# Transposing the normalised x tiles of blocks two to five by DMA instead of on TensorE, in a hybrid short-convolution and chunk-MLP step

## The reference, cut to what matters

```
h = rms_norm(x, g_norm) * (1 + scale) + shift          # scale, shift, gate from silu(c) @ w_ada + b_ada
p = h @ w_in                                           # (T, 1024) @ (1024, 3584)
h_a, b_a, c_a, z_a, u_b, v_b, z_b = split(p, 7 x 512)
s   = c_a * h_a
y_a = b_a * causal_conv3(s) * silu(z_a)                # depthwise, along T
v_n = layer_norm(v_b, g_v, b_v)
y_b = u_b * (tril(W_s) @ v_n + b_s) * silu(z_b)        # in chunks of 128 positions, 8 heads
x + gate * (concat(y_a, y_b) @ w_out)  -> rms_norm(., g_final)
```

## Time and profile before

| | us |
|---|---|
| median of 3 runs | 351.91 (351.71 to 354.35) |
| the profiled execution, time | 349.13 |
| its span, slowest core | 347.5 (345.2 to 347.5) |
| PE busy | 293.0 (84% of the span) |
| DVE busy | 186.2 (54%) |
| ACT busy | 121.5 (35%) |
| POOL busy | 117.3 (34%) |

### The profile page before, as it was taken

The page is one execution under the profiler, slowest core; times in us unless marked ns, Lnnn a source line. Parts: engine busy times, 40 slices in busy tenths (PEclk is TensorE's granted clock), DMA queues, the critical chain, the costliest instruction groups (busy, mean ns, idle before and its releaser), DMA issues.

```text
span 347.5 us, 5602 instructions; the slowest of 8 cores (345.2 to 347.5 us)
## 1 busy us (share of the span) xinstructions
PE 293.0 (84%) x1767; PEld 152.8 (44%) x1792; DVE 186.2 (54%) x348; ACT 121.5 (35%) x215; POOL 117.3 (34%) x163
## 2 busy tenths in 40 slices
PE   0327469997999999999999999999999999989720
PEld 0213234444444445444454444455554567845300
DVE  0321025366464654657777655678734577586552
ACT  2511033128353227323455353345342323313120
POOL 7291264123424242412254241224202222232430
PEclk9999859999899999999999999999999999999875
DMA  5999999999999923480163515013540015071313
GB/s 142 222 166 173 165 169 159 185 234 219 171 211 199 164 80 91 119 271 8 60 182 77 167 25 182 2 60 122 122 122 22 10 62 156 27 215 58 123 61 123
DMA packets 14158, 44.52 MB, mean 128 GB/s; under 512 B 1968, under 2 KB 2352, under 8 KB 13104
## 3 DMA queue, kind: packets, MB, share of 16 engines
q0 software_dynamic: 6624, 21.24, 33.6%
q1 hardware_dynamic: 7504, 22.91, 21.8%
HBM read 51.02 MB, written 8.85 MB: 172 GB/s over the span
## 4 chain that ended last, share of the span: by engine, by line
PE 65%; DMA 11%; DVE 8%; issue 6%; POOL 5%; ACT 2%; DVEq 1%; POOLq 0%; ACTq 0%
PE pb L477 37%; PE pb L702 16%; DMA wada<-wada_l 11%; PE pb L592 8%; PE pb L403 1%; PE pb L654 1%; DVE st L607 1%; PE pb L789 1%; ACT vn_bf L622 1%; DVE tmp L532 1%; DVE ob L721 1%; DVE xn L389 1%; DVE spad L514 1%; POOL ob L721 1%; POOL xa L314 1%
## 5 line engine op out<-in xcount | busy, mean ns | idle before, releaser
L477 PE MATMUL pb<-hT,win_bf 128*128 128x512 bf16 (+3 forms) x672 | 127.0, 344 | 0.8 <-ACT vn_bf L622 0.4
L477 PEld LDWEIGHTS pb<-hT,win_bf 128*128 128x128 bf16 x680 | 66.4, 99 | 56.7 <-issue 3.0
L702 PE MATMUL pb<-wout_bf,yT 128*128 128x512 bf16 (+1 forms) x263 | 61.8, 387 | 4.4 <-POOL stat L768 2.1
L477 PE MATMUL pb<-hT,wh 128*128 128x512 bf16 (+3 forms) x276 | 55.4, 362 | 3.7 <-ACT hT L419 3.6
L551 POOL TENSOR_TENSOR yT<-tmp,tmp 128x512 bf16<-128x512 f32 (+3 forms) x20 | 24.7, 1235 | 60.4 <-DVE tmp L546 40.7
L723 ACT ACTIVATE junk<-ob 128x1024 bf16<-128x1024 f32 (+1 forms) x16 | 16.9, 1057 | 80.5 <-DVE ob L721 50.9
L674 POOL TENSOR_TENSOR yT<-tmp,tmp 128x512 bf16<-128x512 f32 (+3 forms) x20 | 22.9, 1147 | 62.5 <-DVE tmp L664 46.0
L702 PEld LDWEIGHTS pb<-wout_bf,yT 128*128 128x128 bf16 (+1 forms) x272 | 26.0, 100 | 34.3 <-issue 6.2
L477 PEld LDWEIGHTS pb<-hT,wh 128*128 128x128 bf16 x280 | 28.2, 102 | 29.0 <-issue 10.0
L532 DVE SCALAR_TENSOR_TENSOR tmp<-spad,pv,tmp 128x512 f32<-128x512 f32 (+2 forms) x40 | 26.7, 667 | 20.4 <-ACT tmp L525 13.1
L592 PE MATMUL pb<-wv_bf,hT 128*128 128x512 bf16 (+1 forms) x132 | 29.6, 379 | 0.2
(11 more groups left out here) (87 smaller groups left out, 270.4 us busy)
## 6 DMA issues: line engine op xcount, KB each, us to landing
y_p<-ob SPq DMA_DIRECT2D x15, 512.0 KB, 2.7
xc<-x_p SPq DMA_DIRECT2D x14, 512.0 KB, 7.7
wada<-wada_l POOLq DMA_DIRECT2D x6, 1024.0 KB, 33.7
xa<-x_p POOLq DMA_DIRECT2D x10, 512.0 KB, 35.0
win_bf<-win_l POOLq DMA_DIRECT2D x17, 256.0 KB, 38.4
xa<-x_p SPq DMA_DIRECT2D x8, 512.0 KB, 6.4
wout_bf<-wout_l POOLq DMA_DIRECT2D x2, 1024.0 KB, 53.3
wh<-winh_l POOLq DMA_DIRECT2D x4, 256.0 KB, 25.4
```

Of the source, the lines that this page charges most:

```text
L477: ii = pe.matmul(bk.t[:, 0:B.N], lhsT=wsl(m, k), rhs=hT[B.h][:, k, 0:B.N], start=(k == 0), stop=(k == 7))
L702: ii = pe.matmul(bk.t[R, :], lhsT=yT[B.y][:, k, ti * 128:ti * 128 + P], rhs=wout_bf[:, n, k, :], start=(k == 0), stop=(k == 7))
```

## The change

For blocks two to five `prep2` is no longer called. A new function `prep2d` issues one DMA on the SP queue that reads `xn` and writes the block's part of `hT` transposed, from SBUF to SBUF. `prep_xn` calls it right behind the DVE instruction; for the first tile of blocks four and five that is left out and the call comes at the end of the block's loop. Block one keeps PE's transposition. The resources that the DMA is recorded as writing are those of the copies before it: the tile's own, and the eight `hTk` that all tiles of a block share.

```diff
-    def prep_xn(B, i):
+    def prep_xn(B, i, now=True):
...
         pst[(B.i, i)] = rn
+        if B.i > 0 and now:
+            prep2d(B, i)
+
+    def prep2d(B, i):
+        ti, P, kind = B.tiles[i]
+        rn = pst[(B.i, i)]
+        dst = hT[B.h][:, :, ti * 128:ti * 128 + P]
+        op("sp", lambda e: e.dma_start(out=dst, in_=xn[rn][0:P, :], transpose=True),
+           r=[("xn", rn)], w=[("hT", B.h, i)] + [("hTk", B.h, k) for k in range(8)], dma=True)
...
             elif j == 3 and b == 1:
                 nxp(prep_sq, 2)
-                nxp(prep2, 0, "act")
...
             if not late:
-                nxp(prep2, j, "act")
                 nxp(prep_xn, j + 1)
...
             if b == 1 and j == 3:
-                nxp(prep2, 1, "act")
                 nxp(prep_xn, 2)
...
             if j == 3 and N2 is not None and b > 0:
-                prep_xn(N2, 0)
+                prep_xn(N2, 0, False)
             GB(B, j)
             if b == 0 and j == 0:
-                nxp(prep2, 0, "act")
-                nxp(prep2, 1, "dve")
...
-            if b == 0 and j == 1:
-                nxp(prep2, 2, "act")
-                nxp(prep2, 3, "dve")
...
             if b == 1 and j < 2:
-                nxp(prep2, 2 + j, "act")
...
+        if N2 is not None and b > 0:
+            prep2d(N2, 0)
```

## The result

The changed kernel takes 391.07 us (387.94 to 392.59, 4 runs) against 352.25 for the kernel before, run beside it: a ratio of 1.108, 95% interval 1.103 to 1.112, **38.8 us slower**. Its profiled execution took 389.83 us, with a span of 388.3 on the slowest core, again core 2.

The account below looks back on a forecast made before the run. PE, busy 84% of the span, was taken as the bound. +25.0 (block two's wait) + 2 (clock) + 1 (block three) - 4.8 (PE's transpositions) = +23.2 on 349.1 = 372.3, 375 for the runs; range 352 to 412, the forecast's own 365 to 384.

Parts of the forecast that it names:

- Side, and what waits for what: Whole kernel: slower, chance 0.80; block two's chained transpositions hold DVE's third xn, ACT and DVE at prep3, and PE.
- slow in itself: Rival, blocks two to four: a transposition takes 10 us or more even in a quiet queue; 389 or 420 us, chance 0.22.
- the landings of 8 to 12 us: Sign, block two: four transposing DMAs one after another from 84 us, each 8 to 12 us from issue to landing.
- the fourth at 116 to 132 us: Sign, block two: ACT and DVE idle at prep3 until the fourth transposition lands, at 116 to 132 us.
- L: Block two: time from a transposing DMA's issue to its landing, taken as 10 us for each of four.
- the 12.9 us: Time of a 512 KB transfer on SP beside the full POOL queue, used to bound L from above.
- The block's start: Block two: fourth tile lands at 123.9 us, so ACT reads the first projection group at 127.0, not 102.0: +25.0 us.
- The clock: Block two's start: after PE's wait of over 20 us part of the matmuls run at 1.2 GHz, not 2.4: +2 us.
- Block three: Transpositions hidden with 11 us to spare, but the third x load stands behind the second: +1 us, between 0 and 4.
- no wait of PE for hT: Sign, block three: four to six us a transposition and PE never waiting for hT.
- Blocks four and five: Transpositions of 4 us have 16 us or more, and SP's stores and loads move by about one transfer: nothing.
- stays covered: Rival, block two: at L = 3 the transpositions hide and prep3 starts where it did; 345 us for runs, chance 0.14.

Follow-up runs that it names:

- e4: Changed kernel with each transposing DMA recorded as writing its own tile only, so not waiting for the previous landing: 384.76 us, ratio 1.097 to the kernel before.
- p2: Changed kernel with block two's four DMAs as plain copies, not transposed, in 128 rows of 2 KB: 373.77 us, ratio 1.067 to the kernel before.
- e1: The change for blocks three to five alone, block two transposed on TensorE as before: 351.23 us, ratio 0.999 to the kernel before.
- c2: e1 with block three's two x loads issued ahead of its first two transposing DMAs, chain of landings kept: 347.58 us, ratio 0.985 to the kernel before.
- b1: e1 without the chain of landings and with block three's two x loads issued ahead of its first transposing DMAs: 345.33 us, ratio 0.987.
- p1: Changed kernel with block two's four DMAs as plain copies, not transposed, in 1024 rows of 256 bytes: 380.62 us, ratio 1.088 to the kernel before.

## Why the prediction was right, and where not

- **Side, and what waits for what: right.** The four transpositions of block two form a chain, the third xn waits for a landing, ACT and DVE stand at `prep3`, PE stops for the banks and then for hT. All of it stands in the profile after. Which link costs was not right: I had four equal ones, and it is the first (e4: the chain itself is worth 4 us).
- **The number: partly luck.** 391 lies in the range of 352 to 412, but 16 us over the 375 and outside the forecast's own 365 to 384. The range reached that far only for the rival "slow in itself", whose mechanism did not occur. Of the signs, the landings of 8 to 12 us and the fourth at 116 to 132 us did not come true (it landed at 138.8).
- **The step that was mis-sized: L, the price of a transposition beside the full queue.** I took 10 us by interpolating between two loads by their *bytes*: four times 10. It measured 42.4, 3.05, 3.03 and 3.9, together 52.3 instead of 40. p2 is the kernel that my number described: the same bytes in rows of 2 KB took 12.6, 11.3, 10.7 and 2.7 us and gave 374. The transposition has eight times the rows. A single price for all four also hid that the long one outlives the queue, so that the others are cheap. The trace of the kernel before held the price already. In the view that the 12.9 us came from, two loads of 128 KB, queued behind the two of 512 KB, took 24.2 and 28.4 us; so 12.9 was no upper bound. And from 96 to 102 us the queues exchanged packet for packet there too:

```profile
gv_bc<-g_v SPq DMA_DIRECT2D x1, 128.0 KB, 24.2
bv_bc<-b_v SPq DMA_DIRECT2D x1, 128.0 KB, 28.4
...
q0 software_dynamic: 109, 0.79, 71.4%
q1 hardware_dynamic: 108, 0.44, 28.1%
```

  109 turns in 6 us on 16 engines are 0.88 us each, with SP's packets at 4 KB; 64 rows at that are 56 us, an estimate above the 42 measured, but on the right side of 10.
- **The block's start.** I had +25.0 us; it was 39.5. The four landings give 12.3 us of the difference, and xn the other 2.2, as it was that much later here (85.30 against 83.10). PE waited 8.0 us in three pieces for `win_bf`, inside the stretch that was lost anyway.
- **The clock: right.** +2 was forecast. Block two's first group on `wh` took 13.7 us to the next one (139.53 to 153.18) where it took 12.1 before. The window 110 to 133 us (columns as in the earlier trace rows), in which PE did nothing, shows 0.54 of the full clock, close to the lower of its two levels (1.2 of 2.4 GHz), and 139 to 147 us, block two's first, 0.77, where the earlier trace rows had 0.81 after 1.7 us of idle:

```profile
110.00:133.00 23.00, 0.00 (x0) 0.00 (x0) 2.02 (x3) 0.00 (x0) 0.00 (x0) 0.54 0.72 116
...
139.00:147.00 8.00, 7.47 (x28) 3.14 (x29) 3.68 (x9) 4.57 (x7) 1.26 (x1) 0.77 0.80 166
```

- **Block three: the place was right, the size too small.** The x load behind the second transposition was named, with +1 between 0 and 4. PE waited 1.84 and 2.98 us, and then ran 52 matmuls in 11.68 us where e1 has 10.00: some 6.5, outside the 0 to 4. The sign "no wait of PE for hT" failed here, though the first three transpositions took only 3.1 to 3.8 us (the fourth 7.8). e1 shows such waits too (2.45 and 1.01 us), and c2 that this load is most of them.
- **Blocks four and five: right.** Nothing waits; their starts move closer by 1.5 us. c2 and b1, with the nine transpositions off PE's list, are 5.4 and 4.9 us below the kernel before, where 4.8 were counted for PE (in the profiled executions, from block two's start on, 3.6 and 2.8).
- **The rival "slow in itself"** gave 389 with a time that fits, and is wrong: from block two's second tile on a transposition took 3 to 8 us. The Trainium skill's 1309 ns for each piece (VectorE: DVE Perf Modes, the three transpose paths), by estimate 10.5 us a tile, fits no tile here. The 3.0 us of the rival "stays covered", an estimate from the Trainium skill's DMA: Bandwidth & Descriptors, latency and other measured facts, fit most tiles in a quiet queue, at 3.0 to 3.9. Beside the full queue it was out by a factor of fourteen. The same page of the Trainium skill says, under queues, rings and completion order, that each DMA engine takes turns between the queue rows at packet granularity; the 167 and 164 packets above agree. It gives 9 to 17 descriptors as a typical packet. Here the profile counted each 256-byte row as a packet of its own (p1 shows 1,040 of SP's packets from 84 us to its first copy's landing, 1,024 rows and one more for each engine), and such packets were exchanged one for one; that is what makes the turns cost 42 us.

## What to carry to other kernels

Price a DMA that shares the engines with a full queue by its rows for each engine times the time of one of the other queue's packets, not by its bytes: here 64 rows at 0.57 us, and some 4 us before the first row moved. Look for both queues' packet counts in the trace before the change. A transposition by DMA is a good trade for TensorE time where the queues are quiet and nobody waits for it (b1 and c2 gained 1.3 and 1.5% with nine of them), and a bad one while weights stream in. When a DMA that waits joins an in-order queue, put the loads that others need ahead of it.

## What the runs showed of the hardware that was not expected

- Two queues on the same 16 DMA engines exchanged packet for packet, 167 against 164 in 6 us, though POOL's carried 7 KB each and SP's 256 bytes. The bytes went 1.17 MB against 0.04.
- A transposing DMA of 256 KB from SBUF to SBUF took 3.0 to 3.9 us from issue to landing in a quiet queue, a plain copy of the same bytes 2.7 (2 KB rows) and 2.9 us (256-byte rows): without rivals the rows cost almost nothing.
- SP was busy 1.26 us (median) in issuing one transposition, against 0.61 for the plain copy in 1024 rows and 0.48 in 128.
